# Second output projection: three of its four operand groups turned by VectorE and DMA; turned blocks sent in one DMA and sorted by four reads

## The reference, cut to what matters

```python
y_a = sigmoid(ml_o) * rmsnorm(mlstm(...)) * silu(ml_z)      # 256 x 1024
y_b = rmsnorm(hgrn2(...)) * silu(hg_g)                      # 256 x 1024
y = concatenate([y_a, y_b], axis=-1)                        # 256 x 2048
h = h + y @ w_out                                           # the second output projection
gate = sigmoid(rmsnorm(h, pe_norm_w) @ w_pg)
h = h + gate * (p @ w_pe)
out = rmsnorm(h, final_norm_w)
```

## Time and profile before

| | |
|---|---|
| median of 3 runs | 1939.37 us (1938.89 to 1939.51) |
| the profiled execution | 1939.18 us, its span 1937.2 us |
| TensorE clock granted, mean | 0.999 |
| busy: PE / PEld / DVE / ACT / POOL | 1925.4 / 1602.6 / 1240.2 / 970.5 / 17.8 us |
| HBM | 388.86 MB read, 25.17 MB written |

### The profile page before, as it was taken

The page is one execution under the profiler, slowest core; times in us unless marked ns, Lnnn a source line. Parts: engine busy times, 40 slices in busy tenths (PEclk is TensorE's granted clock), DMA queues, the critical chain, the costliest instruction groups (busy, mean ns, idle before and its releaser), DMA issues.

```text
span 1937.2 us, 21917 instructions
## 1 busy us (share of the span) xinstructions
PE 1925.4 (99%) x8738; PEld 1602.6 (83%) x8738; DVE 1240.2 (64%) x1231; ACT 970.5 (50%) x921; POOL 17.8 (1%) x31
## 2 busy tenths in 40 slices
PE   9999999999999999999999999999999999999998
PEld 7888888888888888888888888888889888888886
DVE  7747647745676654444466666677587869676665
ACT  6334444445445444444455555555555546544444
POOL 0000000000000000000000000000000000000000
PEclk9999999999999999999999999999999999999999
DMA  9876977775867388888886555565578544556763
GB/s 320 253 230 180 256 265 212 233 241 192 251 210 262 110 241 242 235 254 237 241 237 217 191 189 192 194 228 183 184 220 246 197 164 157 173 174 225 215 217 109
DMA packets 397670, 415.49 MB, mean 214 GB/s; under 512 B 194812, under 2 KB 225792, under 8 KB 396928
## 3 DMA queue, kind: packets, MB, share of 16 engines
q1 hardware_dynamic: 396552, 412.50, 68.2%
q10 hardware_dynamic: 1016, 1.59, 0.2%
HBM read 388.86 MB, written 25.17 MB: 214 GB/s over the span
## 4 chain that ended last, share of the span: by engine, by line
PE 94%; DVE 3%; ACT 2%; issue 2%; POOL 0%; POOLq 0%; DVEq 0%; ACTq 0%
PE acc L1517 90%; PE mis L1517 3%; ACT hi L568 1%; DVE m L932 1%; DVE lo L950 1%; PE mis L1520 1%; ACT at L597 0%; DVE at L984 0%; ACT m L557 0%; DVE m L940 0%; DVE xs L932 0%; DVE m L1222 0%; ACT xs L557 0%; DVE sm L940 0%; POOLq L1818 0%
## 5 line engine op out<-in xcount | busy, mean ns | idle before, releaser
L1517 PE MATMUL acc<-hi,at 128*128 128x512 f32 (+1 forms) x5344 | 1654.7, 389 | 0.3 <-DVE lo L950 0.3
L1517 PEld LDWEIGHTS acc<-hi,at 128*128 128x128 f32 x5344 | 1000.6, 188 | 202.3 <-DVE lo L950 1.0
L950 DVE TENSOR_TENSOR lo<-raw,hi 128x2048 fp32r<-128x2048 f32 (+1 forms) x333 | 752.9, 2263 | 539.1 <-ACT hi L568 538.8
L1517 PE MATMUL acc<-lo,at 128*128 128x512 f32 (+1 forms) x2672 | 1032.4, 387 | 0.0
L568 ACT ACTIVATE hi<-raw 128x2048 fp32r<-128x2048 f32 (+1 forms) x333 | 628.6, 1891 | 522.2 <-PE acc L1517 488.4
L1517 PEld LDWEIGHTS acc<-lo,at 128*128 128x128 f32 x2672 | 501.9, 188 | 99.3
L557 ACT ACTIVATE m<-acc,st 128x512 f32<-128x512 f32 (+2 forms) x104 | 69.7, 670 | 93.0 <-PE acc L1517 92.2
L932 DVE TENSOR_TENSOR m<-m 128x256 f32<-128x256 f32 (+1 forms) x145 | 75.0, 517 | 20.9 <-ACT m L557 16.2
L557 ACT ACTIVATE m<-m 128x512 f32<-128x512 f32 (+4 forms) x71 | 58.2, 819 | 53.1 <-DVE m L932 37.9
L991 DVE TENSOR_TENSOR at<-m,at 128x1024 fp32r<-128x1024 f32 x64 | 77.9, 1218 | 2.8 <-ACT at L608 2.8
L608 ACT ACTIVATE at<-m 128x1024 fp32r<-128x1024 f32 x64 | 66.7, 1042 | 7.5 <-PE acc L1517 7.5
(11 more groups left out here) (123 smaller groups left out, 466.3 us busy)
## 6 DMA issues: line engine op xcount, KB each, us to landing
raw<-in_w_in SPq DMA_DIRECT2D x133, 1024.0 KB, 5.2
raw<-in_w_up SPq DMA_DIRECT2D x64, 1024.0 KB, 6.2
raw<-in_w_down SPq DMA_DIRECT2D x64, 1024.0 KB, 5.0
raw<-in_w_out SPq DMA_DIRECT2D x32, 1024.0 KB, 5.2
m<-turned SPq DMA_DIRECT2D x36, 512.0 KB, 6.3
raw<-in_w_pg SPq DMA_DIRECT2D x16, 1024.0 KB, 5.1
turned<-m SPq DMA_DIRECT2D x224, 64.0 KB, 3.4
raw<-in_w_in SPq DMA_DIRECT2D x12, 688.0 KB, 4.9
```

What stands on the lines that cost most here:

```text
L950: e.tensor_tensor(lo, raw, hi.bitcast(F32), ALU.subtract).then_inc(s_lo.on("lo", n))
L1517: return e.matmul(o, a, b, start=start, stop=stop)
```

## The change

- y 0, 1, 2 are turned in way (b): y 0 and y 1 out of VM at step 302 behind `ya` (four block transposes of 128x256 each), y 2 out of HV at step 303 (two of 128x512). Their heads land in m at 17, 21 and 25 KB, and SyncE waits for `ya` before it overwrites there. TensorE's units y 0 to 2 are gone.
- Their unit work: ScalarE makes the high part with four activations of 128x256 whose scale is the norm's weight, VectorE the low part with four multiply-subtracts; behind chunks 305, 306, 307 instead of 304, 305, 306. y 3 stays as it was.
- For all turns: the transposed blocks go to DRAM as they lie in one DMA (rows of 2 KB), and four reads of 32 partitions each pick the 32x32 blocks in order (pieces of 128 bytes).
- The load of NF moves from SyncE's step 309 to 324.

```diff
@@ sync: every turn
                     if n == m_ + 6:
                         for t in range(2):
                             sp.wait_ge(s_dve, "turned", j, t)
-                            z = turned_rows[j].rearrange("(c i) k -> i c k", i=32)
-                            for a in range(4):
-                                i, k = slice(32 * a, 32 * a + 32), slice(t * P + 32 * a, t * P + 32 * a + 32)
-                                load(z[:, :, k], turned_to(j, t)[i, :].rearrange("p (c k) -> p c k", c=16), "blocks", j)
+                        load(turned_rows[j].rearrange("(t p) c -> p t c", p=P), both(j), "blocks", j)
                     if n == m_ + 7:
                         sp.wait_ge(loaded("blocks", j), "blocks", j)
-                        load(heads_of(j), turned_rows[j].rearrange("(h p) k -> p h k", p=P), "heads", j)
+                        if j == ("y", 0):
+                            sp.wait_ge(s_dve, "ya", 1, 1)
+                        z = turned_rows[j].rearrange("(a i) (h c k) -> c i h a k", i=32, c=4, k=32)
+                        for c in range(4):
+                            load(heads_of(j)[32 * c:32 * c + 32].rearrange("p h (a k) -> p h a k", k=32), z[c], "heads", j)
...
-                if n == 309:
+                if n == 324:
@@ plan
+        turns_of.update({("y", g): N_RES - 6 + g // 2 for g in range(3)})
...
-        fill_early("y", N_RES - 4, [(N_RES + 2, 0), (N_RES + 2, 1)])
+        fill_early("y", N_RES - 3, [(N_RES + 2, 0), (N_RES + 2, 1)])
@@ scalar, unit
+                if name == "y" and g < 3:
+                    if t == 0:
+                        ac.wait_ge(loaded("heads", (name, g)), "heads", (name, g))
...
+                        ac.wait_ge(s_prod, "products", taken(name, g), 1)
+                        for k in range(4):
+                            c = C_NW + 4 * g + k
+                            e.activation(ATH[:, 4 * g + k, :], heads_of((name, g))[:, k, :], ACT.Copy, scale=COL[:, c:c + 1]).then_inc(
+                                s_ach.on("ath", name, g, t))
+                    return
@@ vector, unit_low
+                if name == "y" and g < 3:
+                    if t == 0:
+                        dv.wait_ge(s_ach, "ath", name, g, t)
+                        for k in range(4):
...
+                            e.scalar_tensor_tensor(ATL[:, 4 * g + k, :], heads_of((name, g))[:, k, :], COL[:, c:c + 1],
+                                                   ATH[:, 4 * g + k, :].bitcast(F32), ALU.mult, ALU.subtract).then_inc(
+                                s_dve.on("atl", name, g, k // 2))
+                    return
@@ vector, turn
+                    if own == "y" and i < 2:
+                        for h in range(2):
+                            then()
+                            e.transpose(turned_to(j, t)[:, S * h:S * h + S], VM[:, t, 2 * i + h, 0:S]).then_inc(
+                                s_dve.on("turned", j, t) if h else s_dve.on())
+                        continue
...
+                    elif own == "y":
+                        src = HV[:, t, 0:512]
@@ tensor, unit
-                if name in ("heads", "x") or name in ("mix", "pg") and g < 3:
+                if name in ("heads", "x") or name in ("mix", "y", "pg") and g < 3:
                     return
```

More of the change, by code:

```diff
@@ L181, in program @@
         XT, PRE = m(32, 4096).rearrange("p (k s) -> p k s", k=16), M[:, 32 * KB - 16:32 * KB]
-        TURNED = [XS[:, i // 4, 512 * (i % 4):512 * (i % 4) + 512] for i in range(8)]
         XSQ = XS.rearrange("p t d -> p (t d)").rearrange("p (k s) -> p k s", k=16)
@@ L314, in program @@
             beside(296 + h, "ml", h)
-        for g in range(2):
-            beside(302, "ya", g)
         beside(316, "p_parts")
@@ L319, in program @@
         turns_of.update({("ut", j): N_UP + 4 * j + 5 for j in range(16)})
+        turns_of.update({("y", g): N_RES - 6 + g // 2 for g in range(3)})
         turns_of.update({("pg", g): N_RES + 4 * g + 4 for g in range(3)})
+        for g in range(2):
+            beside(302, "ya", g)
         for j, n in turns_of.items():
@@ L340, in program, with both, turned_to @@
         freeing = {"heads": N_AB - 4, "mix": N_WO - 4, "r1": N_UP - 4, "r2": N_IN2 - 4, "y": N_RES - 4, "pg": N_PG - 5}
-        def turned_to(j, t):
+        def both(j):
             if isinstance(j, tuple):
                 own, g = j
-                return m({"mix": 24 + 4 * (g % 2), "ut": 68 + 4 * (g % 2), "pg": 48 + 4 * (g % 2)}.get(own, 4 * g) + 2 * t, 512)
-            return TURNED[(2 * (j if j < 4 else j - 2) + t) % 8]
+                z = m({"mix": 24 + 4 * (g % 2), "ut": 68 + 4 * (g % 2), "y": (48, 52, 32)[g % 3], "pg": 48 + 4 * (g % 2)}.get(own, 4 * g), 1024)
+            else:
+                i = (j if j < 4 else j - 2) % 4
+                z = XS[:, i // 2, 1024 * (i % 2):1024 * (i % 2) + 1024]
+            return z.rearrange("p (t c) -> p t c", t=2)
+        def turned_to(j, t):
+            return both(j)[:, t, :]
         def heads_of(j):
             if isinstance(j, tuple):
-                if j[0] in ("mix", "pg"):
-                    return m((32 if j[0] == "mix" else 16) + 4 * j[1], 1024).rearrange("p (h s) -> p h s", h=4)
+                if j[0] in ("mix", "y", "pg"):
+                    return m({"mix": 32, "y": 17, "pg": 16}[j[0]] + 4 * j[1], 1024).rearrange("p (h s) -> p h s", h=4)
                 if j[0] == "ut":
@@ L368, in program @@
         held = {}
-        turned_rows = {j: nc.dram_tensor(f"turned{i}", (512, S), F32, kind="Internal").ap() for i, j in enumerate(turns_of)}
+        turned_rows = {j: nc.dram_tensor(f"turned{i}", (S, 512), F32, kind="Internal").ap() for i, j in enumerate(turns_of)}
         da_p_rows = [nc.dram_tensor(f"da_p{u}", (S, P), F32, kind="Internal").ap() for u in range(8)]
@@ L575, in unit @@
                         x_high(k)
+                    return
+                if name == "y" and g < 3:
+                    if t == 0:
+                        ac.wait_ge(loaded("heads", (name, g)), "heads", (name, g))
+                        ac.wait_ge(loaded("col"), "col")
+                        ac.wait_ge(s_prod, "products", taken(name, g), 1)
[3 more added lines that the diff above has]
+                                s_ach.on("ath", name, g, t))
                     return
@@ L1551, in unit @@
                 if name == "y":
[L1552 to L1555, removed]
+                    pe.wait_ge(s_dve, "g", 1, t)
                 if name == "pg":
@@ L1558, in unit @@
                 src = MX if name == "mix" else XS if name != "y" else HV
-                k0 = 4 * (g % 2) if name == "y" else 4 * g
+                k0 = 4 if name == "y" else 4 * g
                 def part(c):
-                    if name == "y" and g < 2:
-                        return VM[:, t, 2 * g + c // 2, c % 2 * P:(c % 2 + 1) * P]
                     return src[:, t, (k0 + c) * P:(k0 + c + 1) * P]
```

## The result

21 runs of the changed kernel have a median of 1941.75 us (1937.34 to 1946.15), 21 of the kernel before 1939.24 us (1938.82 to 1939.80); the ratio is 1.0013 with an interval of 1.0007 to 1.0019. It is slower by 2.5 us, inside the 0.2% that were called "no change", but on the other side of what was forecast, and its runs spread over 9 us where those of before lie within 1 us. The profiled execution took 1940.19 us (span 1938.2), 1.0 us more than that of before.

The account below looks back on a forecast made before the run. TensorE was taken as the bound, busy 1925.4 of 1937.2 us. The terms -2.7 - 0.3 + 0.9 + 1.5 = -0.6 us on 1939.18 gave 1938.6 us (1938.8 on the median's scale), range 1936.3 to 1942.5 us.

Parts of the forecast that it names:

- Part 1: TensorE, behind chunks 304 to 306: three groups of eight transposes go, 2.7 us saved.
- Part 2: Old TensorE wait at chunk 310: shorter unit work on ScalarE and VectorE, 0.3 us saved if nothing new is late.
- Part 3: VectorE's new turns ahead of low 305 and low 306: TensorE waits at chunk 306, 0.9 us lost.
- Part 4: SyncE's queue and the DMA: late data of y 2 make chunk 310 wait, 1.5 us taken between 0.2 and 8.2.
- the bounds of 4.50 and 7.25: Microseconds a turn's four reads hold SyncE's queue; data of y 2 in place about 1738 or 1746.
- given back exactly: Rival: the wait at chunk 310 is 2.5 to 4 us and eats the gain, 1939.8 to 1941.5 us; chance 0.17.
- The queue rival: SyncE's queue in front of y 2: chunk 310 waits 8.2 us, +6.1 us in all, 1945.5 us; chance 0.13.
- The rule against the change: Skill's rule to transpose 128x128 on TensorE, block transposes only for 32x32: by it the time would come out slower.

Follow-up runs that it names:

- seven: Changed kernel with turn y 2 at step 304, its parts behind chunk 308, its reads behind weights 311: 1937.70 us, ratio 0.9999.
- experiment two: Changed kernel with the old eight sends and one read put back for all turns: 1941.14 us, ratio 1.0012 against the kernel before.
- five: Changed kernel with the high and low parts of y 2 made behind chunk 308 instead of 307: 1939.85 us, ratio 1.0002.
- eleven: As seven, but SyncE reads y 2 one step earlier, ahead of weights 311: 1937.68 us, ratio 0.9993 against the kernel before.
- experiment one: Kernel before with only the new sends (one send, four reads) for the 36 old turns: 1939.02 us, ratio 1.0000.
- eight: The changed kernel run again unaltered, for a second profile and its spread: 1941.99 us.
- nine: Kernel before with four extra VectorE operations ahead of low 310, its DMAs untouched: 1943.77 us, ratio 1.0022.
- thirteen: As eleven, but the send of y 2 is issued by ScalarE's DMA queue: 1937.27 us, ratio 0.9990 against the kernel before.
- Twelve: As eleven, with 8 small unused TensorE products ahead of the products of chunk 310: 1937.18 us, ratio 0.9990 against the kernel before.

## Why the prediction was wrong

The sum said 0.6 us faster, and the kernel is 2.5 us slower. Two terms made the difference: the wait at chunk 310, taken at 1.5 us, was 2.7 us or more, which alone turns the sum to +0.6; and nothing stood in it for the clock behind such a wait.

- **Part 1** held: 24 transposes fewer, and the stretch without them is shorter by what the chain said. In the profile with no wait at 306 and little at 310 (seven) the time is 1936.67 us, 2.5 us under the kernel before.
- **Part 2** held in its durations: the new units take 1.7 us on ScalarE and 2.05 us on VectorE (1.6 and 2.1 were taken). That the old 0.3 us was saved no run shows, since a longer wait stands in its place; the sum comes out the same.
- **Part 3** held to 0.1 us: low 306 was to end at 1726.3 and ended near 1726.5; 0.9 us of wait was said and 0.92 measured. Seven shows that it hangs on turn y 2.
- **Part 4** is the term that failed by its size. "I take 1.5 us, nearer the quick end, since four issues stand in place of eight": it was 2.7 us in one profile and 3.7 in another. The eight reads of y 0 and y 1 took 10.4 us of the queue, 5.2 a turn, between the bounds of 4.50 and 7.25, as foreseen. But the data of y 2 came at 1740.9, against 1738 and 1746 at the bounds, and I had taken them at 1739.3. Of the 2.9 us between 1738 and 1740.9, about 1.7 come from the reads of y 0 and y 1 and 1.5 from the landing, taken at 2 us: the reads of y 2 were issued by 1737.4 and their data came 3.5 us later; the reads of y 2 themselves took 0.3 us less than 4.50. The number of issues was the wrong reason: experiment two has eight sends a turn and loses the same. The list of what stands behind the data (10.7 us, and 10.8 measured) was right, but Part 4 followed only these data. Weights 309 and 310 were late in the same queue too: behind low 309 as it ran, even data at 1738 would have left a wait of about 1.6 us, not 0.2, and experiments five and eleven are held by weights 310 and 309. The move of NF was costed at nothing; no wait of TensorE appears where it went, but no run moved it alone, so that stays untested. That the new sends of the old turns cost nothing is shown by experiment one.
- **A term was missing**: the fall of the granted clock behind a wait, 1.3 us (eight) to 1.6 us (nine) in the profiles that have it. With a wait of 2.7 us alone the changed kernel stands at 1940.2; with 3.7 us and the fall at 1942.0, close to its medians of 1941.75 and 1941.99. The Trainium skill (TensorE: Matmul & The Clock Gate, Why this matters for your kernels) warns of drops to the lower clock mid-kernel after idle gaps of TensorE. The traces agree in kind, but the length of the wait alone does not decide it (falls behind 2.4, 3.2 and 3.7 us, none behind 2.7 and 2.9). I had not weighed it, since no wait of that kind stood in the kernel before.
- **The rivals.** The third, "given back exactly", with a wait of 2.5 to 4 us and 1939.8 to 1941.5 us, is what happened in kind; its upper end lacks the clock. It had 0.17. The queue rival had the right place and a third to a half of its price.
- **The rule against the change** came out right in sign: as placed, VectorE's transposes and the DMA behind them cost more than TensorE's eight at 0.89 us a group. Placed otherwise (eleven to thirteen) they are worth 1.5 to 2.1 us, so it is a matter of the stretch and not of the operation.

Twelve and thirteen are faster than the kernel before, by 2.1 and 2.0 us, and so than the changed one; eleven, by 1.5 us, is not clear of the noise (0.9984 to 1.0002). What remains open is how each of the transfers between 1718 and 1745 shares the engines; the run-to-run difference of a landing was seen in two profiles only.

## What to carry to other kernels

Work moved off the bound engine pays only if what it displaces is not in time by a hair: list the in-order work behind each wait it adds (here copies, gating and a low part, 10.7 us in series behind one landing) and move the consumer behind it before anything else. Follow every transfer behind the new ones in the same queue, not only the new data: here weight loads came late as well, and once the data were moved, the weights set the time. Price a new wait of the size seen here (2.4 us and up) on TensorE at its length plus the slow stretch that may follow, and look at the spread of the runs as well as at one profile: it showed a loss that the first profile did not have.

## What was not expected of the hardware

- The granted clock fell to half behind single waits of 2.4, 3.2 and 3.7 us, with products at 0.43 instead of 0.23 us, and did not behind waits of 2.7 and 2.9 us. Held at the same place by VectorE alone, nine of eleven runs were 1.2 us or more above the length of the wait.
- Small products without a use, put into a wait, made the kernel 1.8 us faster (1941.99 to 1940.22).
- A send of 512 KB in rows of 2 KB landed within 4.0 us of its issue when reads stood just ahead of it in the queue (the changed kernel), and within 7.2 us when a weight load did (eleven); from ScalarE's queue it was 5.1 us at most.
